# Decay rows inside the FoX score product, two heads scored ahead of the last value piece, pool products ahead of the values, a new depth order of the output projection

## The chip, the cores and the metric

One NeuronCore of a Trainium2 chip runs the whole program. The metric is the device time of one execution in microseconds (us), and the time of a kernel is the median of its runs.

## The reference

The reference is a two-layer decoder trunk over 256 tokens of width 1024. Each layer runs a token mixer, cross-attention into 256 memory tokens, and a SwiGLU channel mixer (dense in layer 0, the best 2 of 8 experts in layer 1). Every sub-layer has an RMSNorm before and after it. The change touches the token mixer only:

```python
proj = hn @ w_in
sq, sk, sv, fq, fk, fv, f_logit, u = jnp.split(proj, SPLIT_POINTS, axis=-1)
sb   = stick_breaking_attention(sq, sk, sv)             # 6 heads of 64
log_f_cum = cumsum(log_sigmoid(f_logit + b_forget))     # one row per FoX head
# FoX head: softmax_s( (q_t . k_s)/8 + log_f_cum[t] - log_f_cum[s] ), s <= t, times v
fox  = forgetting_attention(fq, fk, fv, log_f_cum)      # 6 heads of 64
pool = multiscale_pool(u, pool_w, pool_scale)           # 4 causal windows, 64 channels each
return concatenate([sb, fox, pool]) @ w_out
```

A stick-breaking head takes z = q.k/8, forms log_keep = -softplus(z) below the diagonal, sums it over the later keys, and weights the values with exp(log_sigmoid(z) + that sum).

## The kernel before

**Stages and banks.** Every product of a layer is a stage of tiles of 256 columns, listed in `STAGES` (L64); a mixer layer runs mixT (transposed, normalised tokens), u (pool input), f (forget logits), fqk and sqk (queries and keys, transposed), v (values, 6 tiles), the heads, pool (2 tiles), out (8 tiles). `ORDER` (L69) numbers the tiles, and tile n uses PSUM bank n mod 8. `pieces` (L1650) issues a stage on TensorE: per tile eight depth blocks `k` of 128, each three matmuls (high x high, high x low, low x high parts of the fp32 operands, L1626 to L1628 in `product`). ScalarE and VectorE move finished tiles out of PSUM, alternately (`take`, L774 and L1161; `plain_tile`, L405).

**Weights.** A weight piece (1 MB, two tiles) goes by DMA from SyncE's queue into one of six raw buffers. ScalarE writes its fp32r high part and VectorE the low part (`split`, L732 and L1156, the operations L730 and L1152), each into one of three buffers. `split_behind` places the split of piece c+3 behind the moves of piece c's tiles. SyncE waits at piece 14 (the first of xk) until the heads are mixed, then loads the post-norm gain, the memory tokens, and piece 14 on (L617 to L620).

**Heads.** `heads` stands once on TensorE (L1676), once on ScalarE (L809) and once on VectorE (L1215); each engine works in its own written order, and semaphores tie them together. In iteration i:

- TensorE: the scores of FoX head i (L1689: queries x keys over 64 rows; L1692: `decay_q` x `decay_k` over 128 rows, which adds the two decay terms to the same bank), the scores of stick-breaking head i (L1697, L1698), the sums of head i-1 (L1706 to L1708), the transposes of the FoX probabilities of head i-1 (L1714), the value products of head i-2 (L1726, L1727).
- ScalarE: Abs, Exp, Ln of head i (L816 to L818), the two softmax exponentials (L821), the Exp of the stick-breaking weights of head i-1 (L827), the move of its transposed probabilities (the helper L730), and in every second iteration the high parts of a finished pair (L730 again, output `rows`).
- VectorE: mask and row maximum of FoX head i (L1224, L1227), keep terms (L1231, L1233), reciprocal and scaling (L1235, L1237), the logarithms of the weights of head i-1 (L1246), and in every second iteration the low parts of a pair (L1152, output `rows`).

Six heads of each kind run through this in eight iterations per layer. TensorE enters `heads` after all v tiles are moved; ScalarE and VectorE enter it behind the moves of v and behind the split that `take_all` puts after the last v tile. `decay_q` and `decay_k` lie in `xn`; GpSimd clears them and writes the constant rows (L662 to L666), VectorE writes the decay rows in `decay` (L1201).

**After the heads.** TensorE waits for `sb_mix` and `fox_mix` (the last low parts), runs the two pool products (L2042), waits until both pool tiles are split (`wait_moved`, L2044), and begins `out`, whose tiles take the depth blocks in the order 0 to 7. Blocks 0 to 2 are stick-breaking pairs, 3 to 5 FoX pairs, 6 and 7 the pool. GpSimd prepares the pool input (L677 to L687) and signals `pool_ready`.

## Time and profile before

| | us |
|---|---|
| median of 3 runs | 1666.8 |
| lowest and highest run | 1658.07, 1669.35 |
| the profiled execution | 1652.1 |
| its span, first to last instruction | 1650.3 |
| mean granted TensorE clock in the span | 0.98 |

The profile comes from one execution. Its times count from the start of the span; a busy time is the time an engine spends in instructions, and "idle before" is its pause ahead of an instruction with the engine that ended it. The first layer's mixer lies at about 5 to 145 us, the second's at about 475 to 600 us. Matmul ends are modelled, so differences between starts are firmer than single durations. In a timeline "xN" counts records; a plain fp32 matmul has two.

### The profile page before, as it was taken

The numbers are of one execution on the slowest core, as the hardware profiler recorded it, in microseconds if no ns is written. First come the engines' busy times: TensorE is split into PE (matmuls) and PEld (weight loads), VectorE is DVE, ScalarE is ACT, GpSimd is POOL, SyncE is SP. The second block draws the span as 40 slices with busy tenths as digits, with TensorE's granted clock in tenths as the row PEclk, the third lists the DMA queues.
The fourth block names the chain that finished last, engine by engine and source line by source line (L and its number), as shares of the span: only waits on it lengthen the run. The fifth ranks groups of instructions, "written<-read, shape, count | busy, mean of one in ns | idle before, by whom it ended". The sixth has DMA issues, their size and how long they took to land.

```text
span 1650.3 us, 23029 instructions
## 1 busy us (share of the span) xinstructions
PE 1508.8 (91%) x9225; PEld 1301.8 (79%) x9225; DVE 1102.0 (67%) x1052; ACT 962.3 (58%) x1108; POOL 131.9 (8%) x125
## 2 busy tenths in 40 slices
PE   6989988999979899879999998989898899999986
PEld 6969978999979699779997676666666799866664
DVE  4556545444555565466776888878798676778886
ACT  5356445334353664354445787868778454478776
POOL 6100000000040000001001002020200200100200
PEclk9999998999989999979999999999999999999998
DMA  9318523555633085334667999999999667689993
GB/s 312 113 60 260 184 85 128 179 182 189 200 102 103 25 270 192 115 103 154 230 230 241 322 382 341 377 352 347 385 341 374 232 222 246 236 288 382 354 370 146
DMA packets 224150, 385.79 MB, mean 234 GB/s; under 512 B 11924, under 2 KB 114680, under 8 KB 223880
## 3 DMA queue, kind: packets, MB, share of 16 engines
q1 hardware_dynamic: 223072, 382.12, 66.3%
q8 instruction: 83, 1.36, 0.3%
q10 hardware_dynamic: 424, 1.08, 0.2%
q0 software_dynamic: 512, 0.74, 0.2%
q14 instruction: 59, 0.48, 0.1%
HBM read 382.85 MB, written 1.05 MB: 233 GB/s over the span
## 4 chain that ended last, share of the span: by engine, by line
PE 74%; DVE 12%; ACT 8%; issue 4%; DMA 1%; ACTq 0%; SPq 0%; DVEq 0%
PE banks L1626 12%; PE banks L1627 12%; PE banks L1628 12%; DVE w_low L1152 9%; PE banks L1624 8%; PE banks L1625 7%; PE banks L1937 6%; ACT w_high L730 5%; PE banks L1939 5%; PE banks L1881 2%; PE banks L1873 2%; PE banks L1832 1%; PE banks L1818 1%; DVE after_heads L1424 1%; ACT rows L730 1%
## 5 line engine op out<-in xcount | busy, mean ns | idle before, releaser
L1152 DVE TENSOR_TENSOR w_low<-raw,w_high 128x2048 fp32r<-128x2048 f32 x357 | 808.2, 2292 | 302.7 <-ACT w_high L730 295.9
L730 ACT ACTIVATE w_high<-raw 128x2048 fp32r<-128x2048 f32 x357 | 679.9, 1915 | 279.1 <-PE banks L1939 102.0
L1624 PE MATMUL banks<-w_high,rows 128*128 128x512 f32 (+1 forms) x576 | 224.4, 396 | 30.9 <-DVE w_low L1152 20.9
L1626 PE MATMUL banks<-rows,w_high 128*128 128x256 f32 x832 | 238.3, 286 | 12.2 <-DVE rows L1153 8.6
L1627 PE MATMUL banks<-rows,w_high 128*128 128x256 f32 x832 | 237.6, 286 | 0.0
L1628 PE MATMUL banks<-rows,w_low 128*128 128x256 f32 x832 | 237.4, 285 | 0.0
L1625 PE MATMUL banks<-w_low,rows 128*128 128x512 f32 (+1 forms) x576 | 213.3, 377 | 1.5 <-issue 1.5
L1937 PE MATMUL banks<-rows,w_high 128*128 128x320 f32 x704 | 186.4, 310 | 8.3 <-DVE w_low L1152 5.6
L1939 PE MATMUL banks<-rows,w_low 128*128 128x256 f32 x704 | 184.6, 279 | 0.0
L1626 PEld LDWEIGHTS banks<-rows,w_high 128*128 128x128 f32 x832 | 162.0, 195 | 14.2 <-issue 13.7
L1624 PE MATMUL banks<-w_high,eT 128*128 128x512 f32 x352 | 144.3, 410 | 20.4 <-DVE w_low L1152 13.6
L1624 PEld LDWEIGHTS banks<-w_high,rows 128*128 128x128 f32 x576 | 109.2, 190 | 67.9 <-issue 38.9
L1627 PEld LDWEIGHTS banks<-rows,w_high 128*128 128x128 f32 x832 | 162.1, 195 | 0.4
L1628 PEld LDWEIGHTS banks<-rows,w_low 128*128 128x128 f32 x832 | 161.9, 195 | 0.0
L1626 PE MATMUL banks<-w_high,rows 128*128 128x256 f32 x480 | 136.5, 284 | 5.1 <-DVE rows L1152 2.8
L1937 PEld LDWEIGHTS banks<-rows,w_high 128*128 128x128 f32 x704 | 132.8, 189 | 9.3 <-issue 9.3
L1625 PE MATMUL banks<-w_low,eT 128*128 128x512 f32 x352 | 138.9, 395 | 0.0
L1627 PE MATMUL banks<-w_low,rows 128*128 128x256 f32 x480 | 135.8, 283 | 0.0
L1628 PE MATMUL banks<-w_high,rows 128*128 128x256 f32 x480 | 135.8, 283 | 0.0
L1939 PEld LDWEIGHTS banks<-rows,w_low 128*128 128x128 f32 x704 | 134.0, 190 | 0.5 <-issue 0.5
L1625 PEld LDWEIGHTS banks<-w_low,rows 128*128 128x128 f32 x576 | 109.4, 190 | 22.4 <-issue 5.5
L1624 PEld LDWEIGHTS banks<-w_high,eT 128*128 128x128 f32 x352 | 66.0, 188 | 64.7 <-issue 38.3
(200 smaller groups left out, 2028.8 us busy)
## 6 DMA issues: line engine op xcount, KB each, us to landing
raw<-in_moe_w_gate_dram SPq DMA_DIRECT2D x176, 512.0 KB, 5.4
raw<-in_moe_w_up_dram SPq DMA_DIRECT2D x176, 512.0 KB, 5.6
raw<-in_moe_w_down_dram SPq DMA_DIRECT2D x176, 512.0 KB, 5.4
raw<-in_w_in_dram SPq DMA_DIRECT2D x40, 512.0 KB, 6.1
raw<-in_xa_wkv_dram SPq DMA_DIRECT2D x32, 512.0 KB, 8.5
raw<-in_dense_w_gate_dram SPq DMA_DIRECT2D x22, 512.0 KB, 4.4
raw<-in_dense_w_up_dram SPq DMA_DIRECT2D x22, 512.0 KB, 4.2
raw<-in_dense_w_down_dram SPq DMA_DIRECT2D x22, 512.0 KB, 3.6
```

Of the source, the lines that this page charges most:

```text
L730: return act.activation(out_, in_, ACT.Copy, scale=scale)
L1152: return dve.tensor_tensor(out_, in_, plain(high), ALU.subtract)
L1424: dve.tensor_tensor(both, both, banks[:, at:at + blocks, 0:width(s)], ALU.mult).then_inc(hidden_ready, 1)
L1624: pe.matmul(dst, stay[0], move[0], start=start, stop=False, skip_group_check=True)
L1625: return pe.matmul(dst, stay[0], move[1], start=False, stop=stop, skip_group_check=True)
L1626: pe.matmul(dst, stay[0], move[0], start=start, stop=False, skip_group_check=True)
L1627: pe.matmul(dst, stay[0], move[1], start=False, stop=False, skip_group_check=True)
L1628: return pe.matmul(dst, stay[1], move[0], start=False, stop=stop, skip_group_check=True)
L1873: pe.matmul(banks[:, bank_of(half, s, blocks - 1, blocks), 0:width(s)], fold, low_rows[:, half, 0:width(s)], start=False, stop=True, skip_ ...
L1881: ins = pe.matmul(dst[:, j, b * P:(b + 1) * P], inner[:, b, j * P:(j + 1) * P], twice if stacked(b) else ident, start=True, stop=True)
L1937: pe.matmul(dst[:, 0:2 * n].rearrange("p (h s) -> p h s", h=2), w_h[:, k, cols], x[:, :, 0:n], start=(i == 0 and k == 0), stop=False, skip ...
L1939: ins = pe.matmul(dst[:, 0:SEQ], w_l[:, k, cols], x[:, 0, :], start=False, stop=(i == of_step(s) - 1 and k == per - 1), skip_group_check=True)
```

## The change

Six edits, in both layers:

1. **FoX scores in one product.** `fox_q` and `fox_k` have 128 rows per head: 64 rows of queries or keys, and in the other half the decay rows, ones and zeros. `plain_tile` moves each fqk tile in two halves of 64 rows into them. One pair of products replaces L1689 and L1692. GpSimd clears four strided halves and writes two sets of ones, VectorE's `decay` writes 12 rows instead of 7.
2. **Order inside a head's scores.** The stick-breaking scores come ahead of the FoX scores on TensorE (`head_front`).
3. **Two heads ahead.** The fronts of heads 0 and 1 run on all three engines after v tile 3, ahead of v tiles 4 and 5. `heads` begins at iteration 1. The split behind v tile 3 goes between the two fronts, the split behind v tile 5 behind the heads. Banks are counted from the first pool tile (`head_bank`).
4. **Where TensorE waits for v.** It waits for v tiles 0 and 1 ahead of the fronts and for all v tiles ahead of iteration 2.
5. **Pool products** move from behind the heads to between sqk and v, with their moves.
6. **Depth order of out:** 0, 1, 3, 4, 6, 7, 2, 5. The waits for the last `sb_mix` and `fox_mix` stand ahead of blocks 2 and 5 of its first tile.

```diff
-STAGES = [("mixT", 4), ("u", 2), ("f", 1), ("fqk", 6), ("sqk", 6), ("v", 6), ("pool", 2), ("out", 8),
+STAGES = [("mixT", 4), ("u", 2), ("f", 1), ("fqk", 6), ("sqk", 6), ("pool", 2), ("v", 6), ("out", 8),
...
+MIXED_IN_ORDER = [k for k in range(KT) if k % PAIRS < PAIRS - 1 or k >= 2 * PAIRS] + [PAIRS - 1, 2 * PAIRS - 1]
...
-        decay_q = view(flat_xn, 0, HEADS, SEQ)
-        decay_k = flat_xn[:, HEADS * SEQ:(HEADS + 1) * SEQ]
+        fox_q = view(flat_xn, 0, HEADS, SEQ)
+        fox_k = view(phase, 0, HEADS, SEQ)
...
+            if stage == "fqk":
+                for h in (2 * (i % PAIRS), 2 * (i % PAIRS) + 1):
+                    ins = move((fox_q if i < PAIRS else fox_k)[own_rows(h), h, :], src[own_rows(h), :],
+                               HD ** -0.5 if i < PAIRS else 1.0)
+                return ins
...
+        def own_rows(h):
+            return slice(HD * (h % 2), HD * (h % 2) + HD)
+        def decay_rows(h, at):
+            first_row = HD - HD * (h % 2) + at
+            return slice(first_row, first_row + HEADS)
+        def head_bank(layer, b):
+            return banks[:, (tile(layer, "pool") + b) % BANKS, :]
...
-                chain(pool.memset(flat_xn[:, 0:(HEADS + 1) * SEQ], 0.0))
+                for odd in range(2):
+                    for t in (fox_q, fox_k):
+                        chain(pool.memset(t[own_rows(1 - odd), odd:HEADS:2, :], 0.0))
                 for h in range(HEADS):
-                    chain(pool.tensor_scalar(decay_q[32:32 + HEADS, h, :], ones[32:32 + HEADS, :],
...
+                    at = decay_rows(h, 32)
+                    chain(pool.tensor_scalar(fox_q[at, h, :], ones[at, :], ident[at, at.start + h:at.start + h + 1], None,
+                                             ALU.mult))
+                chain(pool.memset(fox_k[decay_rows(0, 0), 0:HEADS:2, :], 1.0))
+                pool.memset(fox_k[decay_rows(1, 0), 1:HEADS:2, :], 1.0).then_inc(decay_set, 1)
...
 # ScalarE and VectorE
-                take_all(layer, "v")
+                take_all(layer, "pool")
+                take_all(layer, "v", 0, 3)
+                take(layer, "v", 3)
+                head_front(layer, 0)
+                split_behind(layer, "v", 2)
+                head_front(layer, 1)
+                take_all(layer, "v", 4, last_split=False)
                 heads(layer)
-                take_all(layer, "pool")
+                split_behind(layer, "v")
                 take_all(layer, "out")
...
 # TensorE
+                        if stage == "out" and i == 0 and k in (PAIRS - 1, 2 * PAIRS - 1):
+                            pe.wait_ge(sb_mix if k == PAIRS - 1 else fox_mix, PAIRS * (layer + 1))
...
+            def head_front(layer, i):
+                rows, c, n = own_rows(i), i // 2, HEADS * layer + i
+                sq, sk = (qkT[rows, PAIRS * m + c, :] for m in (2, 3))
+                b = head_bank(layer, 2 + i % 3)
+                pe.matmul(b[:, 0:SEQ], sk[:, 0:P], sq, start=True, stop=False, skip_group_check=True)
+                pe.matmul(b[:, SEQ:TRI], sk[:, P:SEQ], sq[:, P:SEQ], start=False, stop=False,
+                          skip_group_check=True).then_inc(sb_scored, 1)
+                b = head_bank(layer, i % 2)
+                if i >= 2:
+                    pe.wait_ge(fox_masked, n - 1)
+                for t, cols, keys in ((0, slice(0, P), P), (1, slice(P, TRI), SEQ)):
+                    ins = pe.matmul(b[:, cols], fox_q[:, i, t * P:(t + 1) * P], fox_k[:, i, 0:keys], start=(t == 0),
+                                    stop=(t == 1), skip_group_check=True)
+                ins.then_inc(fox_scored, 1)
...
+                    if i == 1:
+                        wait_moved(pe, after(layer, "v"))
...
-                pieces(layer, "v", x_parts)
-                if layer == 0:
-                    pe.wait_ge(consts_in, 16)
-                heads(layer)
                 pe.wait_ge(pool_ready, layer + 1)
...
                 for c in range(COUNT["pool"]):
                     pe.matmul(bank(tile(layer, "pool", c))[:, 0:SEQ], poolw[:, layer, c, :], pool_r[:, c, :],
                               start=True, stop=True).then_inc(tile_full, 1)
-                wait_moved(pe, after(layer, "pool"))
+                pieces(layer, "v", x_parts, of=range(4))
+                wait_moved(pe, tile(layer, "v", 2))
+                pe.wait_ge(decay_ready, layer + 1)
+                head_front(layer, 0)
+                head_front(layer, 1)
+                pieces(layer, "v", x_parts, of=range(4, COUNT["v"]))
+                heads(layer)
                 pieces(layer, "out", mix_parts)
```

ScalarE's and VectorE's `head_front` are the lines that stood under `if i < HEADS` of their `heads`, with `head_bank` for the bank. The loops of `heads` run over i = 1 to 7 and call it for i from 2 to 5.

## Rows read from the trace of the kernel before

**Rows 1.** The page, part 4: chain that ended last, by engine.

```profile
PE 74%; DVE 12%; ACT 8%; issue 4%; DMA 1%; ACTq 0%; SPq 0%; DVEq 0%
```

**Rows 2.** Windows, layer 0's heads: length, busy (xcount) PE, PEld, DVE, ACT, POOL, clock, DMA, GB/s.

```profile
79.50:117.70 38.20, 32.91 (x178) 23.37 (x179) 23.82 (x75) 24.53 (x64) 0.00 (x0) 1.00 0.03 9
```

**Rows 3.** Timeline, ScalarE, moves of v tiles 3 and 5: start, us, instruction, idle before.

```profile
73.49 0.38 ACT L730 ACTIVATE phase<-banks 128x256 f32<-128x256 f32 x1 [3.58 <-PE banks L1628]
...
79.24 0.38 ACT L730 ACTIVATE phase<-banks 128x256 f32<-128x256 f32 x1 [3.57 <-PE banks L1628]
```

**Rows 4.** Critical chain, 55 to 125 us: start, us, what.

```profile
79.52 1.91 ACT w_high L730
81.46 2.29 DVE w_low L1152
...
88.06 0.85 PE banks L1692 x4
...
98.02 0.85 PE banks L1689 x4
...
103.41 0.85 PE banks L1689 x4
```

**Rows 5.** Timeline, start of the heads on TensorE and VectorE.

```profile
79.73 0.89 PE L1689 MATMUL banks<-phase 64*128 64x128 f32 x4 [0.52 <-issue]
...
81.40 0.48 PE L1697 MATMUL banks<-phase 64*128 64x256 f32 x1
...
81.42 0.49 PE L1689 MATMUL banks<-phase 64*128 64x128 f32 x2
...
85.89 0.55 DVE L1237 TENSOR_SCALAR phase<-phase,small 128x128 f32<-128x128 f32 x2
```

**Rows 6.** Timeline, ScalarE's Abs of heads 1 to 5, layer 0.

```profile
85.56 0.47 ACT L816 ACTIVATE phase<-banks 128x384 f32<-128x384 f32 x1
...
90.41 0.48 ACT L816 ACTIVATE phase<-banks 128x384 f32<-128x384 f32 x1
...
95.21 0.49 ACT L816 ACTIVATE phase<-banks 128x384 f32<-128x384 f32 x1
...
100.60 0.49 ACT L816 ACTIVATE phase<-banks 128x384 f32<-128x384 f32 x1
...
106.00 0.49 ACT L816 ACTIVATE phase<-banks 128x384 f32<-128x384 f32 x1 [0.55 <-PE banks L1698]
```

**Rows 7.** Timeline, one round of ScalarE and VectorE between two Abs.

```profile
92.04 0.56 DVE L1231 SCALAR_TENSOR_TENSOR phase<-banks,phase 128x384 f32<-128x384 f32 x1 [1.58 <-ACT phase L818]
...
93.76 0.55 DVE L1246 TENSOR_TENSOR phase<-banks,cst 128x384 f32<-128x384 f32 x1
...
94.35 0.52 ACT L827 ACTIVATE phase<-phase 128x384 f32<-128x384 f32 x1 [1.47 <-DVE phase L1246]
```

**Rows 8.** Timeline, TensorE from the last values to the first out tile.

```profile
114.11 0.38 PE L1727 MATMUL banks<-phase 128*64 128x128 f32 x2
115.47 1.10 PE L2042 MATMUL banks<-res,poolw 128*128 128x256 f32 x4 [0.98 <-DVE rows L1152]
117.70 0.35 PE L1626 MATMUL banks<-w_high,rows 128*128 128x256 f32 x1 [1.13 <-issue]
```

**Rows 9.** Timeline, GpSimd in layer 0's mixer, first and last step.

```profile
21.80 1.60 POOL L662 MEMSET xn<- 128x1792 f32 x1 [12.49 <-DMA cst<-in_constants_dram]
...
46.55 0.74 POOL L687 TENSOR_TENSOR res<-res 64x256 f32<-64x256 f32 x1
```

**Rows 10.** Timeline, SyncE's queue: the load of the memory tokens.

```profile
115.84 0.43 SPq L620 DMA_DIRECT2D phase<-in_mem_dram  x1
```

**Rows 11.** The memory tensor: time from issue to landing, both layers.

```profile
DMA to landing us min/median/max: 6.5/7.4/8.3
```

**Rows 12.** Timeline, ScalarE's first use of the memory tokens, layer 0.

```profile
130.38 1.06 ACT L745 ACTIVATE xn<-phase 128x1024 f32<-128x1024 f32 x1
```

**Rows 13.** Timeline, ScalarE's Abs of head 5, layer 1.

```profile
563.30 0.49 ACT L816 ACTIVATE phase<-banks 128x384 f32<-128x384 f32 x1 [0.55 <-PE banks L1698]
```

More of the change, by code:

```diff
@@ L828, in heads @@
                         act.wait_ge(fox_turned, n + 1)
[L829 removed]
+                        move(fox_pT[:, j % 2, :], head_bank(layer, 5)[:, 0:TRI]).then_inc(fox_pt, 1)
                     if i >= 2 and i % 2 == 1:
@@ L1241, in heads @@
+            def heads(layer):
+                for i in range(1, HEADS + 2):
+                    if 2 <= i < HEADS:
+                        head_front(layer, i)
+                    if i <= HEADS:
                         j, n = i - 1, HEADS * layer + i - 1
@@ L1648, in turn_stage, with pieces @@
                             ins.then_inc(tile_full, 1)
-            def pieces(layer, stage, tokens=None, x=x_parts, turned=None):
-                for i in range(COUNT[stage]):
+            def pieces(layer, stage, tokens=None, x=x_parts, turned=None, of=None):
+                for i in range(COUNT[stage]) if of is None else of:
                     if (stage, i) == ("out", 6):
```

150 lines of the change are left out of this document (70 added, 80 removed).

## The prediction

> **What bounds the kernel now.** I read the chain that ended last first. TensorE holds 74% of it, VectorE 12%, ScalarE 8%, DMA 1% [rows 1]. So a change counts where it shortens TensorE's work, or a place where TensorE waits for the two others. The next view is the table by windows. In the value stage ScalarE waits 3.58 and 3.57 us for TensorE at each second tile, and two tiles take 5.75 us [rows 3]: that stage is bound by products. The heads are another kind of stage: in 38.2 us TensorE is busy 32.9, VectorE 23.8, ScalarE 24.5, and DMA 3% [rows 2]. No engine is full, so the end is set by turns between engines, and the timelines must be read.
>
> They show three parts in layer 0. (a) The start. V ends at 79.2 (79.73 less the 0.52 of pause) [rows 5], and the first thing ScalarE and VectorE do is the split behind it, 1.91 and 2.29 us, until 83.75 [rows 4]. The chain runs through it, so both heads' elementwise work stands behind it. (b) The rounds. TensorE's own round is 103.41 - 98.02 = 5.39 us [rows 4]. ScalarE's Abs come at 85.56, 90.41, 95.21, 100.60, 106.00: steps of 4.85, 4.80, 5.39, 5.40. Only the last waited for TensorE by the view (0.55 us) [rows 6]. (c) The end. The last value product ends at 114.49 (114.11 + 0.38), the pool products wait until 115.47, and out begins at 117.70 [rows 8].
>
> The second layer does the same 457.3 us later (563.30 against 106.00) [rows 6, 13], so each saving counts twice.
>
> **Why the rounds have a second bound.** Between two Abs stand, one behind the other: Abs, Exp, Ln on ScalarE (VectorE's L1231 waits 1.58 us for them), then four VectorE steps up to L1246 at 93.76, then L827 at 94.35, which waited 1.47 us for L1246, then a move and the next Abs at 95.21 [rows 6, 7]. That is a ring of 4.80 us in which TensorE's products have no part as long as scores and sums come in time. A round with a pair's high parts is longer by 5.39 - 4.80 = 0.59.
>
> **The change part by part (layer 0, times on the scale of before).**
>
> Decay rows in the score product. L1692 goes, 0.85 us of TensorE per head [rows 4]. What replaces L1689 has 128 rows instead of 64. No row shows this product itself; the nearest are L1689 over 64 rows and L1692 over 128, both 0.85 for the same columns [rows 4]. So I take 0.85 saved, with the other end at 0 (the joined product costs as much as both; it replaces them with half the instructions, which excludes a loss). TensorE's round becomes 5.39 - 0.85 = 4.54. The ring of 4.80, or 5.39 with a pair, then binds. Of six times 0.85 = 5.1 us nearly all is lost to it: in the rounds that end with Abs 3, 4 and 5 the ring gives 4.80, 5.39, 4.80 against 4.80, 5.39, 5.40, a saving of **0.6**.
>
> Here a rule speaks against the joining. L1697 of head 0 (rows 0 to 63) and L1689 of head 1 (rows 64 to 127) start 0.02 us apart [rows 5]: they run side by side. The Trainium skill (TensorE: Matmul & The Clock Gate, The mechanism) says that products in different row groups of the array run at the same time. The trace agrees. A product over all 128 rows can share with nobody, so by the rule the two first fronts took five slots of 0.85 before and take four now: one slot less, not two.
>
> More rows for others. Every fqk tile is moved in two halves instead of one, VectorE writes five decay rows more, GpSimd makes four half clears for one (1.60 us) [rows 9] and two sets of ones for one. ScalarE's pause of 3.58 us in such stages [rows 3] hides the moves. GpSimd finishes at 47.29 (46.55 + 0.74) [rows 9]; if each new clear costs as much as the whole old one, that is 4.8 us more, some 52. I cost it at 0; what it costs if the cover goes is the third rival.
>
> Pool products first. They take 1.10 us in the trace [rows 8]. Now they stand ahead of v, which TensorE binds, so v tile 3 ends at 79.21 - 5.75 + 1.10 = 74.56 instead of 73.46 [rows 3, 5]. Their moves fall into the pauses of rows 3. The upper end is 1.6, with a pause at the change between kinds of product like the 0.52 of rows 5, the lower 0.9.
>
> Two heads ahead. Fronts begin at 74.56 + 0.52 = 75.08. Stick-breaking scores of head 0 end at 75.93, FoX at 76.78, the second head's at 78.48. V tiles 4 and 5 then run to about 78.8 + 5.75 = 84.5. For head 0 the trace has 85.56 - 83.75 = 1.81 us from VectorE's start on the mask to the end of ScalarE's softmax part [rows 4, 6], so ScalarE is through with it at 76.9 + 1.81 = 78.7 (its Abs, Exp and Ln lie before and beside that). Split of piece 11: high until 80.65, low until 82.95. From the end of the low part (83.75) [rows 4] to the scaled probabilities (86.44) [rows 5] it was 2.69 us with the same work, so head 1 is through at 85.65. Then one v move (0.35) and L1246 of head 0 at 86.0. From L1246 to the next Abs it is 95.21 - 93.76 = 1.45 [rows 6, 7]. Abs 2 comes at 87.45, before at 90.41: **2.95 saved**, pool's 1.10 already paid. TensorE needs for it: v tile 5 done at 84.6, sums and transposes of head 0 (at most 1.5, half of what is left of its round of 5.39 after three groups of 0.85), the scores of head 2, 0.85: 86.9, in time by 0.5. Here is the added wait: ahead of head 2's scores TensorE waits for v tile 4's move, which stands in VectorE's queue behind head 1, at 86.0 by the estimate; behind the wait stand the scores of head 2, and Abs 2 waits for them. The lower end of the saving is 1 (this queue 2 us late), the upper 4 (the split hidden wholly).
>
> The split behind v tile 5 goes behind the heads: 1.91 + 2.29 in ScalarE's and VectorE's queues as out begins. Its piece serves out tiles 4 and 5, two pieces of 5.75 us after out begins; it is done after 4.6. It delays the first tile's post-norm part by some 1.5 us, which nothing waits for before the banks come round, so 0.
>
> The tail. From Abs 5 to the last value product it was 114.49 - 106.00 = 8.49 us, all turns of ScalarE, VectorE and TensorE, and none of them is edited. So it ends at 114.49 - 2.95 - 0.6 = 110.94.
>
> New depth order. Before, 117.70 - 114.49 = 3.21 us lay between the last value product and out. Now out begins at once, with 0.25 for the step. Six blocks of three products at 0.12 us (48 in 5.75) [rows 3] last 2.2 us. The last low part ends TensorE's pause ahead of the pool products, at about 115.4 [rows 8], 0.9 after the values. Block 2, 2.2 behind them, finds it done. **2.95 saved** (2.2 to 3.2).
>
> What goes on behind: the memory tokens' load is released by the end of the heads, 3.55 earlier, but used by ScalarE 6.5 earlier. Issued 115.84, landed 6.5 to 8.3 later, so at 124.1 at worst, used at 130.38 [rows 10 to 12]: the slack shrinks from 6.3 to 3.3 and nothing waits. The weights queue behind this load, so they too come 3 us closer to their use; they would have to be the bound in out or xk to cost anything, and DMA has 1% of the chain [rows 1].
>
> **Sum.** 2.95 + 0.6 + 2.95 = 6.5 us per layer, 13.0 for both. 1652.1 - 13.0 = 1639.1 for the profiled execution (its span 1650.3 and 1.8 around it), a ratio of 0.9921. The median of the runs is 1666.8, 14.7 above that execution; against it the forecast is 1666.8 x 0.9921 = **1653.7**. A measurement of this kernel tells about 1% (16.7 us) from no change, so the likeliest case lies inside "same". Its own range: the bounds of the parts give 1 + 0 + 2.2 to 4 + 0.6 + 3.2, 3.2 to 7.8 per layer, 1651 to 1660.
>
> **Rivals.**
>
> *TensorE binds the rounds after all.* Then each of the four later fronts gives its full 0.85 on top: the chain that ended last does run over TensorE's groups from 88 to 103 [rows 4], which speaks for it. Against: steps of 4.85 and 4.80 in rows 6, where TensorE's round is 5.39, and the 1.47 us waits of L827. It needs a ring shorter than 4.80, for instance since stick-breaking scores come first. Price: rounds of 4.54 against 4.80, 5.39, 4.80, which is 1.4 more, and up to 1.05 at the start, 2.4 per layer: 1653.7 - 4.9 = 1649. Chance 0.15.
>
> *The start gives nothing.* The two fronts only shift the same split (one still lies between them, 4.2 us), and TensorE waits for v tile 4's move in VectorE's queue. Then only 0.6 + 2.95 less pool's 1.10 stays, 2.45 per layer: 1666.8 - 4.9 = 1662. For it: head 1's chain ends at 85.7, after v's end at 84.6, so TensorE has no head work ready beyond head 0's. Against: head 1's whole front was behind 83.75 before and is ready at the same time as head 0's now. Chance 0.17.
>
> *Slower: GpSimd is late for the pool products.* TensorE now needs `pool_ready` ahead of v, at 79.2 - 3 x 5.75 = 61.9, instead of at 115. All products wait behind it. It decides once GpSimd ends later than 61.9 + 6.5 = 68.4 in the first layer: 21 us later than 47.29. Each us beyond costs one. If the six strided clears and ones cost 6 us each instead of 1.6, GpSimd ends about 80: 18 - 6.5 = 11.5 slower in layer 0, about as much in layer 1, 1666.8 + 23 = 1690. The 1.60 us of the whole old clear [rows 9] speaks against it. Chance 0.04.
>
> *The rest*, such as a bank or a weight piece that comes late in out, a few us either way and within 1%: 0.04.
>
> **From these to the numbers.** Forecast 0.60, rivals 0.15, 0.17, 0.04, 0.04. Range: own range 1651 to 1660, widened to the first two rivals and to the spread of a median (runs of before lie 1658 to 1669): 1642 to 1664. Faster by over 1% needs a result below 1650.1: two thirds of the first rival (0.10) and a fifth of the forecast (0.12), where its parts or the median fall low: 0.22. Slower by over 1%: the slower rival, 0.04. Within 1%: the rest, 0.74.
>
> **What would show it.** After: Abs to Abs steps of 4.8, 5.4, 4.8 from head 2 on, none waiting for TensorE; no L1692; L827 still waiting about 1.47 for L1246. From the last value product to the first out product under 0.5 us, with no wait inside out's first tile. From the last sqk product to the first out product 6.5 less than before. Wrong if the Abs steps shrink to the 4.5 of TensorE's round, if TensorE waits over 1 us behind v tile 5, or if a pause stands ahead of the pool products.

## The result, and the profile after

| | before | after |
|---|---|---|
| median | 1663.6 us (4 runs) | 1642.2 us (4 runs) |
| lowest and highest run | 1658.07, 1669.35 | 1640.05, 1643.27 |
| profiled execution, its span | 1652.1, 1650.3 | 1643.3, 1641.4 |
| mean granted clock in that span | 0.980 | 0.972 |

The ratio is 0.9869, 95% interval 0.983 to 0.9909. The changed kernel run again beside 23 more runs of before gave 1642.5 us (1641.24 to 1643.0) against 1662.1, ratio 0.9884 [0.9858, 0.9911]. So the change is worth 1.2 to 1.3%: over 1% in both point values, though both intervals reach to just under 1%. The forecast was 1653.7 and "within 1%" with 0.74; its range of 1642 to 1664 begins where the result lies.

The two spans differ by 8.9 us only. They are single executions, and the one of before, at 1652.1, was faster than all four runs in the table. So the comparison is made piece by piece inside layer 0's mixer, where both traces have the full clock.

First TensorE's timeline of the changed kernel, from the pool products (L2084) through the two fronts (L1728, L1729 the stick-breaking scores, L1736 the joined FoX score product) to the first full round. Columns: start, us, instruction, idle before and what ended it.

```profile
61.90 1.02 PE L2084 MATMUL banks<-res,poolw 128*128 128x256 f32 x4
62.57 0.47 PE L1670 MATMUL banks<-w_high,rows 128*128 128x256 f32 x1
...
74.35 0.70 PE L1728 MATMUL banks<-phase 64*128 64x256 f32 x2
...
76.90 0.92 PE L1736 MATMUL banks<-phase,xn 128*128 128x128 f32 x4
77.47 0.47 PE L1670 MATMUL banks<-w_high,rows 128*128 128x256 f32 x1
...
85.44 0.67 PE L1728 MATMUL banks<-phase 64*128 64x256 f32 x2 [0.68 <-DVE phase L1179]
...
89.76 0.70 PE L1728 MATMUL banks<-phase 64*128 64x256 f32 x2
...
90.61 0.92 PE L1736 MATMUL banks<-phase,xn 128*128 128x128 f32 x4
91.37 0.59 PE L1750 MATMUL banks<-phase,cst 128*128 128x256 f32 x2
...
94.11 0.70 PE L1728 MATMUL banks<-phase 64*128 64x256 f32 x2
```

To be seen: from the first pool product to the next product of v it is 62.57 - 61.90 = 0.67 us, though the group is drawn 1.02 long (ends are modelled, starts are firm). The fronts begin at 74.35 without a pause and end at 77.47, 3.12 for two heads. In a round the joined product takes 91.37 - 90.61 = 0.76. After v the only wait is 0.68 us, for the move of v tile 4 (L1179), which stands in VectorE's queue behind head 1. TensorE's own round is 94.11 - 89.76 = 4.35.

ScalarE's Abs of the six heads and the Exp of the stick-breaking weights (L853) of one round:

```profile
75.31 0.49 ACT L837 ACTIVATE phase<-banks 128x384 f32<-128x384 f32 x1 [0.46 <-PE banks L1729]
79.86 0.46 ACT L837 ACTIVATE phase<-banks 128x384 f32<-128x384 f32 x1
86.59 0.48 ACT L837 ACTIVATE phase<-banks 128x384 f32<-128x384 f32 x1
91.33 0.48 ACT L837 ACTIVATE phase<-banks 128x384 f32<-128x384 f32 x1
95.26 0.52 ACT L853 ACTIVATE phase<-phase 128x384 f32<-128x384 f32 x1 [1.47 <-DVE phase L1282]
96.59 0.50 ACT L837 ACTIVATE phase<-banks 128x384 f32<-128x384 f32 x1
101.34 0.48 ACT L837 ACTIVATE phase<-banks 128x384 f32<-128x384 f32 x1
```

They answer to [rows 6, 7]. The steps from head 2 on are 4.74, 5.26, 4.75, where TensorE's round is 4.35: none of these three Abs waits for TensorE, and L853 waits for VectorE as before. The sum of the mixer, from the first out product (L1670) backwards, on TensorE:

```profile
101.59 0.52 PE L1758 MATMUL banks<-cst,phase 128*128 128x128 f32 x3 [0.49 <-ACT phase L754]
...
104.17 0.70 PE L1750 MATMUL banks<-phase,cst 128*128 128x256 f32 x2 [0.62 <-DVE phase L1264]
...
106.32 0.52 PE L1758 MATMUL banks<-cst,phase 128*128 128x128 f32 x3 [1.01 <-ACT phase L754]
107.05 0.62 PE L1773 MATMUL banks<-phase 128*64 128x256 f32 x2 [0.21 <-DVE rows L1184]
...
109.44 0.38 PE L1774 MATMUL banks<-phase 128*64 128x128 f32 x2
109.76 0.39 PE L1670 MATMUL banks<-w_high,rows 128*128 128x256 f32 x1
```

The first out product comes 117.70 - 109.76 = 7.94 us earlier than in [rows 8]. By pieces:

| piece of layer 0 | forecast | measured | from |
|---|---|---|---|
| start: third head's Abs | 2.95 | 3.82 | 90.41 against 86.59 |
| rounds: from there to the sixth Abs | 0.6 | 0.84 | 15.59 against 14.75 |
| tail: to the start of the last value product | 0 | 0.01 | 8.11 against 8.10 |
| end: from there to the first out product | 2.95 | 3.27 | 3.59 against 0.32 |
| sum | 6.5 | 7.94 | |

These are times from the start of the span, and the two executions do not reach the values at the same time. In before the first product behind sqk, the first of v, is this one; in after it is the pool product at 61.90, 0.13 later:

```profile
61.77 0.28 PE L1626 MATMUL banks<-w_high,rows 128*128 128x256 f32 x1
```

Counted from there the saving is 7.94 + 0.13 = 8.07 us. In layer 1, where the same products start at 519.07 and 512.85, it is (575.01 - 519.07) - (560.70 - 512.85) = 8.09, with Abs steps of 6.74, 4.73, 5.26, 4.75. So the mixers give 16.2 us. By layer 1's first out product the profiled execution is 575.01 - 560.70 = 14.3 us ahead, and at its end only 8.9. It has the lower mean granted clock, 0.972 against 0.980, and has lost some us in stretches at half clock. One of them stands at the start of xk (the keys of the memory tokens) in layer 0, behind a pause that before had too:

```profile
136.62 0.36 PE L1670 MATMUL banks<-rows,w_high 128*128 128x256 f32 x1 [1.82 <-issue]
...
137.68 0.42 PE L1670 MATMUL banks<-rows,w_high 128*128 128x256 f32 x1
137.89 0.41 PE L1671 MATMUL banks<-rows,w_high 128*128 128x256 f32 x1
...
140.70 0.28 PE L1670 MATMUL banks<-rows,w_high 128*128 128x256 f32 x1
140.82 0.28 PE L1671 MATMUL banks<-rows,w_high 128*128 128x256 f32 x1
```

From start to start it is 0.21 us, later 0.12. The same products in the trace of before, behind the same pause of 1.82 us, are at 0.12 at once:

```profile
144.53 0.35 PE L1626 MATMUL banks<-rows,w_high 128*128 128x256 f32 x1 [1.82 <-issue]
...
145.31 0.28 PE L1626 MATMUL banks<-rows,w_high 128*128 128x256 f32 x1
145.43 0.28 PE L1627 MATMUL banks<-rows,w_high 128*128 128x256 f32 x1
```

GpSimd, which the third rival was about, has four half clears of 0.73 for the one of 1.60 [rows 9] and ends at 50.7 instead of 47.3, 11 us before TensorE needs the pool input:

```profile
21.53 0.73 POOL L684 MEMSET xn<- 64x768 f32 x1 [11.75 <-DMA cst<-in_constants_dram]
...
24.75 7.48 POOL L687 TENSOR_SCALAR xn<-cst 6x256 f32<-6x256 f32 x6
...
32.29 0.73 POOL L689 MEMSET phase<- 6x768 f32 x1
...
48.04 2.67 POOL L711 TENSOR_TENSOR res<-res 64x256 f32<-64x256 f32 x1
```

### The profile page after: what moved, and what is told of

Same layout as the page of the kernel before. It is cut to its first block, busy times and chain, and to the rows that moved or that the text cites. A ratio compares the mean times of both kernels' runs of the same rounds, so it can differ in the third digit from the quotient of the medians.

```text
span 1641.4 us, 22961 instructions
## 1 busy us (share of the span) xinstructions
PE 1509.3 (92%) x9177; PEld 1307.6 (80%) x9177; DVE 1109.4 (68%) x1068; ACT 964.2 (59%) x1114; POOL 147.1 (9%) x133
## 3 DMA queue, kind: packets, MB, share of 16 engines
q8 instruction: 80, 1.31, 0.3%
## 4 chain that ended last, share of the span: by engine, by line
PE 73%; DVE 13%; ACT 10%; issue 4%; DMA 1%; ACTq 0%; SPq 0%; DVEq 0%
PE banks L1670 12%; PE banks L1671 12%; PE banks L1672 12%; PE banks L1668 9%; DVE w_low L1184 8%; PE banks L1669 7%; PE banks L1982 6%; ACT w_high L754 5%; PE banks L1984 5%; PE banks L1918 2%; PE banks L1926 2%; PE banks L1877 2%; PE banks L1863 1%; DVE after_heads L1462 1%; ACT rows L754 1%
## 5 line engine op out<-in xcount | busy, mean ns | idle before, releaser
L1670 PE MATMUL banks<-rows,w_high 128*128 128x256 f32 x832 | 239.0, 287 | 11.9 <-DVE rows L1185 8.3
L1670 PEld LDWEIGHTS banks<-rows,w_high 128*128 128x128 f32 x832 | 162.6, 195 | 13.9 <-issue 13.4
L1670 PE MATMUL banks<-w_high,rows 128*128 128x256 f32 x480 | 137.3, 286 | 2.8 <-DVE rows L1184 2.8
```

Source lines behind the costliest of these rows:

```text
L1670: pe.matmul(dst, stay[0], move[0], start=start, stop=False, skip_group_check=True)
```

## The experiments

In each, the start of the first out product of layer 0 is set against 109.76 of the changed kernel. Where the first head's Abs is later or earlier than 75.31, that offset comes from ahead of the heads and is taken off first; for the two kernels with all of v ahead of the heads it is read from the pool products, which start at 61.90 in the changed kernel. A comparison in layer 0 sees tenths of a us, the medians only whole ones.

### Both kernels again

Before, unchanged, gave 1660.7 (1654.7 to 1667.45, 12 runs), ratio 0.9992 [0.9968, 1.0017]; what after gave stands above. Their expectations:

> The kernel before unaltered, a second profile of it. Theory M: ratio 1.000 within 0.004; first out product at 117.7 us within 0.3; half-clock spells at other places or of other length than in the first profile, and a span that differs from 1650.3 by about half the difference in the length of these spells (mean clock lower by 0.005 goes with some 8 us more). Rival S: spells at the same places and the span within 2 us of 1650.3.

> The changed kernel unaltered, to separate what the edits give from what the runs of both kernels scatter. Theory M (the mixers give 2 x 7.9 us, read from the two profiles between the last sqk product and the first out product; what lies beyond is where TensorE's half-clock spells happen to fall): ratio to before 0.988 to 0.993, i.e. 12 to 20 us, and a profile whose first out product is again at 109.8 us while the later stages differ from the last profile by a few us either way. Rival S (the changed order also removes something systematic behind the mixer, worth 6 us): ratio 0.987 or lower again, and the stages behind the mixer shorter than in before at the same clock.

In the second trace of before the first out product is at 117.30, 0.4 earlier than in the first trace (I had allowed 0.3), as is all ahead of it; in that of after at 109.00, its first Abs at 74.56, both 0.75 earlier. Counted from the first product behind sqk, at 61.37 and 61.15, the second pair gives (117.30 - 61.37) - (109.00 - 61.15) = 8.08 us, the first gave 8.07. Behind the mixers the two pairs differ. The second changed execution is 574.65 - 559.44 = 15.2 us ahead at layer 1's first out product and 1657.4 - 1639.3 = 18.1 at the end, where the first pair had 14.3 and 8.9.

### Two heads ahead, undone

All six v tiles ahead of the fronts, as before the change. With them go both weight splits of v on ScalarE and VectorE, which again stand ahead of the fronts, and edit 4: TensorE waits for all v tiles ahead of the fronts. The four other edits are kept. TensorE's part:

```diff
-                pieces(layer, "v", x_parts, of=range(4))
-                wait_moved(pe, tile(layer, "v", 2))
+                pieces(layer, "v", x_parts)
+                wait_moved(pe, after(layer, "v"))
...
                 head_front(layer, 0)
                 head_front(layer, 1)
-                pieces(layer, "v", x_parts, of=range(4, COUNT["v"]))
```

> The changed kernel with edit 3 undone: fronts of heads 0 and 1 behind v tile 5 and behind its split, all else as changed. Theory M (start 3.8 us per layer of the 7.9): Abs of head 2 within 0.7 us of before's 90.41 on the same scale, first out product 3.5 to 4.5 us later than 109.8, so about 113.8; whole kernel 7 to 9 us slower than the changed one, ratio to before 0.994 to 0.997. Rival (the start gives nothing, the gain comes from the joined product and the order alone): first out product at 110 to 111.

1657.1 us (12 runs), ratio 0.9972 [0.9948, 0.9995]: nearly all of the gain is gone, more than I had put on this edit. The first out product comes at 116.35 (offset -0.20, so 6.8 us later), not at the 113.8 I had expected, and the steps of Abs are 4.23, 4.86, 6.55, 5.45, 4.75. The third head's Abs is already 4.8 late (91.19 + 0.20 against 86.59), and the rounds lose the other 2.0. The timeline of its TensorE shows why:

```profile
83.00 0.92 PE L1728 MATMUL banks<-phase,xn 128*128 128x128 f32 x4
86.51 1.22 PE L1742 MATMUL banks<-phase,cst 128*128 128x256 f32 x2 [2.59 <-DVE phase L1260]
...
89.16 1.22 PE L1720 MATMUL banks<-phase 64*128 64x256 f32 x2
```

and its table by windows (columns as in [rows 2], the clock is third from the right):

```profile
85.00:89.00 4.00, 2.49 (x9) 2.14 (x9) 3.79 (x15) 3.29 (x11) 0.00 (x0) 0.61 0.00 0
89.00:93.00 4.00, 4.00 (x12) 3.10 (x11) 1.86 (x8) 2.43 (x7) 0.00 (x0) 0.50 0.00 0
93.00:97.00 4.00, 4.00 (x17) 2.91 (x16) 2.55 (x9) 1.89 (x6) 0.00 (x0) 0.61 0.00 0
97.00:101.00 4.00, 4.00 (x25) 3.20 (x24) 2.27 (x9) 2.52 (x7) 0.00 (x0) 1.00 0.02 4
```

TensorE is through with both fronts at 83.92, while VectorE is still at the low part of the split (until 84.52). TensorE then has nothing to do for 2.59 us. In this pause, at about 85.9 (the clock is 1.00 from 85.0 to 85.5 and 0.50 from 86.0 on), the granted clock falls to its lower level, 1.2 GHz, and stays there for some ten us: the scores take 1.22 where they take 0.70 at 2.4 GHz. In the kernel before, TensorE pauses at the same place for 1.71 us, and there the clock stays at 1.00 [rows 2]. (The same pause and the same 1.22 stand in layer 1, at 544.43.) TensorE, with slack in these rounds at full clock, becomes their bound at half. The Trainium skill (TensorE: Matmul & The Clock Gate, Part 1: The HAM clock gate) says that the throttled clock is the default and that activity releases it. This trace agrees: the clock is back at about 96.1, with TensorE busy without a pause since 86.51.

The twelve runs tell the same: seven, with a mean granted clock of 0.962 to 0.966, have a median of 1660.1, and five, at 0.971 to 0.974, one of 1653.0. That fits spells which come in some executions and not in all, and cost some 7 us where they do. It isn't shown, as only one of the twelve was profiled.

Whether the pause is what brings it can be tried. So the same kernel with more work for TensorE: the joined FoX product issued twice, with the same result, since the second one starts the sums anew.

```diff
-                for t, cols, keys in ((0, slice(0, P), P), (1, slice(P, TRI), SEQ)):
-                    ins = pe.matmul(...)
+                for _ in range(2):
+                    for t, cols, keys in ((0, slice(0, P), P), (1, slice(P, TRI), SEQ)):
+                        ins = pe.matmul(...)
```

> The kernel with edit 3 undone (fronts behind v) and the joined product issued twice: more work for TensorE than in that kernel. There TensorE paused 2.59 us behind the two fronts and its granted clock fell to half for about 10 us in the heads of both layers, which put the first out product at 116.35. Clock theory: the 1.7 us of doubled products fill that pause to about 0.9 us, the clock stays at 1.00 through the heads, and the first out product comes at 113.5 to 115.0, earlier than with less work; median 1 to 5 us below that kernel's 1657.1. Rival (the half clock there had another cause): clock again at 0.5 and the first out product at 118 or later.

1650.5 us (8 runs), ratio 0.9949 [0.9927, 0.997]. The first out product is at 113.93 with an offset of -0.63, 2.0 earlier than without the extra products. The median is 6.6 us lower, but the intervals of the two ratios overlap and their series of before had medians of 1662.1 and 1659.7, so the 2.0 is the firmer figure (1.7 in layer 1, counted from its pool products). The pause is now half as long, 1.31 us shorter by two doublings of 0.65, and the clock stays whole:

```profile
83.23 1.58 PE L1729 MATMUL banks<-phase,xn 128*128 128x128 f32 x8
86.08 0.70 PE L1743 MATMUL banks<-phase,cst 128*128 128x256 f32 x2 [1.28 <-DVE phase L1260]
```

```profile
85.00:89.00 4.00, 2.92 (x17) 2.50 (x18) 3.79 (x14) 3.39 (x11) 0.00 (x0) 1.00 0.00 0
89.00:93.00 4.00, 3.77 (x24) 2.82 (x22) 2.41 (x10) 2.97 (x8) 0.00 (x0) 1.00 0.02 4
```

The extra products shorten the pause and also make TensorE busier ahead of it; which of the two keeps the clock up is not separated. Against the changed kernel it is 113.93 + 0.63 - 109.76 = 4.8 us per layer. In the changed kernel itself the doubling costs 1.6 (below), here less, as a part falls into the pause; so edits 3 and 4 together carry between 3.2 and 4.8 at full clock, and they also keep TensorE from that pause.

### The old depth order

The waits stay, ahead of blocks 2 and 5; only the order goes back to 0 to 7.

```diff
-MIXED_IN_ORDER = [k for k in range(KT) if k % PAIRS < PAIRS - 1 or k >= 2 * PAIRS] + [PAIRS - 1, 2 * PAIRS - 1]
+MIXED_IN_ORDER = list(range(KT))
```

> The changed kernel with the depth order of out back to 0 to 7, the waits ahead of blocks 2 and 5 kept, pool products still ahead of v. Block 2 then comes 0.7 us after the last value product instead of 2.2, and the last low parts of both kinds come about 0.9 later than that product. Theory M (most of the 3.2 us between values and out was the pool products and their split standing there): first out product still at 109.8 and a pause inside out's first tile of 0.3 to 0.8 us only, the kernel 0.5 to 1.6 us slower than the changed one in both layers together. Rival (the new depth order carries the saving): 3 us per layer lost, the second tile of out 3 us later.

1643.2 us, ratio 0.9897 [0.9868, 0.9925], first out product at 109.63, and no product of out's first tile waits. The low part of the last stick-breaking pair is done by the time block 2 comes, 0.8 us after the first product. The new order is worth nothing that can be seen. What took 3.27 us from the end is edit 5, the pool products and their split no longer standing there, together with the place of the waits, which this run keeps. In the changed kernel the very last low part is written from here on:

```profile
110.28 0.42 DVE L1184 TENSOR_TENSOR rows<-banks,rows 128x256 fp32r<-128x256 f32 x1 [0.23 <-ACT rows L754]
```

That is until 110.70, 0.94 behind the first out product. Before, TensorE stood still for such a part, 0.98 us ahead of the pool products [rows 8]. So about 1 of the 3.27 belongs to the moved waits and about 2.3 to edit 5. No run undoes either of them alone.

### TensorE's work in the rounds: the joined product twice

The same doubling in the changed kernel. I expected it to put back what edit 1 had taken out, 0.85 us per head.

> The changed kernel with each joined FoX score product issued twice into the same bank (the second overwrites the first, the values stay): it puts back the 0.85 us per head that edit 1 took from TensorE, and nothing else. Ring theory (ScalarE and VectorE bind the rounds at 4.74, 5.26, 4.75): TensorE's round goes from 4.35 to 5.20, the Abs steps of heads 2 to 5 become 5.2 to 5.3 each, the first out product comes at 111.2 to 111.8 instead of 109.8, and the kernel loses 3 to 4 us, far less than 12 x 0.85 = 10.2. TensorE theory (each product on TensorE is paid in full): first out product at 114.9, 10 us lost.

1645.7 us (1638.71 to 1650.28), ratio 0.9918 [0.989, 0.9946]. First out product at 110.94 with an offset of -0.38, so 1.6 per layer later; the steps from the third head on are 5.35, 5.54, 4.76. On TensorE:

```profile
91.54 1.58 PE L1737 MATMUL banks<-phase,xn 128*128 128x128 f32 x8
92.95 0.59 PE L1751 MATMUL banks<-phase,cst 128*128 128x256 f32 x2
```

From start to start the doubled product takes 1.41 where the single one takes 0.76, so the doubling adds 0.65 and not 0.85, and TensorE's own round is 5.00. Of 6 x 0.65 = 3.9 us per layer 1.6, two fifths, are seen. Where a round has 4.75 - 4.35 = 0.4 of slack on TensorE, 0.65 more costs part of itself. It fits the rounds' second bound, and the rival (each product counts in full, here 3.9) falls.

### What the second bound consists of: keep terms without the mask

VectorE's multiplication of the keep terms by the strict mask (L1264, 0.56 us) left out, in the changed kernel and in the one before. The output then misses this masking; the time is of the same program otherwise.

```diff
-                                               in1=sb_l[:, i % 2, :], op0=ALU.max, op1=ALU.add))
-                dve.tensor_tensor(sb_keep[:, i % 2, :], sb_keep[:, i % 2, :], strict, ALU.mult).then_inc(sb_kept, 1)
+                                         in1=sb_l[:, i % 2, :], op0=ALU.max, op1=ALU.add).then_inc(sb_kept, 1)
```

> The changed kernel without the masking of the keep terms (the multiplication by the strictly lower mask on VectorE is left out in every head). Ring theory: the ring shortens by 0.59 us, to 4.15, below TensorE's own 4.35; Abs steps of heads 2 to 5 become 4.35 to 4.4 where no pair's parts are moved and about 4.7 where they are, and the first out product comes 2 to 3 us earlier, near 107.3. TensorE theory: steps unchanged, first out product at 108.6 (only the two times at start and tail where the step stands alone).

> The kernel before with the same masking left out. Ring theory: TensorE's round is 5.40 there, so the rounds give nothing; only one step at the start (TensorE waits for the keep terms of head 0) and one in the tail go: first out product at 116.3 to 116.8 instead of 117.7, half or less of what the same cut gives in the changed kernel. Rival (VectorE binds before as well): 2.5 us or more.

Both expectations missed; each kernel ran once. In the changed kernel the first out product is at 109.49 with an offset of +0.27, 0.5 per layer earlier, and the steps are 4.70, 5.07, 4.62; in the one before the steps do not move (4.85, 4.80, 5.39, 5.40, as in [rows 6]) and the first out product, 117.33 with an offset of -0.19, is 0.2 earlier. VectorE's timeline of the first names the reason:

```profile
93.19 0.56 DVE L1262 SCALAR_TENSOR_TENSOR phase<-banks,phase 128x384 f32<-128x384 f32 x1 [0.38 <-ACT phase L839]
94.06 0.17 DVE L1265 RECIPROCAL small<-small 128x2 f32<-128x2 f32 x1 [0.32 <-ACT phase L842]
```

The reciprocal now waits for ScalarE's softmax exponentials (L842, the last ends at 94.04), which had run beside the keep terms and end nearly as late (in the changed kernel at 93.80, the keep terms at 94.11). The ring is real, but I had the wrong contents for its middle: Abs, Exp, Ln, then on ScalarE the two exponentials with keep terms beside them, then reciprocal, scaling, the logarithms of the weights (L1282), L853, a move, the next Abs. Taking out one of two branches of nearly equal length gives next to nothing.

### The ring made shorter

If so, the way out is to take L1282 out of the chain and not to make a link of it shorter: it needs only the sums of head i-1, which TensorE has long written. VectorE takes it ahead of head i's keep terms.

```diff
+                if i >= 2:
+                    take_sums(layer, i - 1)
...
-                    if i <= HEADS:
-                        j, n = i - 1, HEADS * layer + i - 1
...
-                        dve.tensor_tensor(sb_w[:, j % 2, :], head_bank(layer, 2 + j % 3)[:, 0:TRI], low_min,
-                                          ALU.min).then_inc(sb_logw, 1)
+                    if i <= HEADS and not 2 <= i < HEADS:
+                        take_sums(layer, i - 1)
```

> The changed kernel with one VectorE step moved: L1282 of head i-1 (the logarithms of its weights) comes ahead of the keep terms of head i instead of behind its scaled probabilities. The cut of the masking has shown that the keep terms are not the path: ScalarE's softmax exponentials run beside them and end as late. The ring through them is Abs, Exp, Ln, exponentials, reciprocal and scaling, L1282, L853, move: 4.74. Ring theory, corrected: taken early, L1282 lets ScalarE go on from its exponentials to L853 without the wait of 1.3 to 1.47 us; ScalarE's own round is then 3.5 to 4.2 and TensorE's 4.35 binds, so that the Abs steps of heads 2 to 5 become 4.35 to 4.6, the first out product comes 2 to 3.5 us earlier (106.3 to 107.8), and the kernel gains 4 to 7 us on the changed one's 1642.5. TensorE theory (rounds were bound by its products, nothing to gain): steps 4.74, 5.26, 4.75 as they are.

1637.4 us (1633.54 to 1637.82), ratio 0.9833 [0.9801, 0.9865], 5 us less than the changed kernel, though the intervals of the two just touch; first out product at 107.01 with an offset of +0.39, 3.1 per layer earlier. ScalarE's timeline:

```profile
93.86 0.51 ACT L853 ACTIVATE phase<-phase 128x384 f32<-128x384 f32 x1
...
95.46 0.49 ACT L837 ACTIVATE phase<-banks 128x384 f32<-128x384 f32 x1 [0.17 <-PE banks L1733]
...
99.81 0.49 ACT L837 ACTIVATE phase<-banks 128x384 f32<-128x384 f32 x1 [0.72 <-PE banks L1733]
```

L853 no longer waits, Abs now waits for TensorE, and the steps are 4.12, 4.35, 4.35: the last two are exactly TensorE's own round. Only here does the work that edit 1 removed come through nearly in full: the three steps are 12.82 us together, 2.77 less than in [rows 6], and TensorE's three rounds are 3 x 1.04 = 3.12 shorter.

### The split between the two fronts

The split of piece 11 behind both fronts and behind v tile 4's move, instead of between the fronts.

```diff
+                head_front(layer, 1)
+                take(layer, "v", 4)
                 split_behind(layer, "v", 2)
-                head_front(layer, 1)
-                take_all(layer, "v", 4, last_split=False)
+                take(layer, "v", 5)
```

> The changed kernel with the split of the weight piece behind both fronts instead of between them, and v tile 4's move ahead of it. By the chain that ended last the start runs through this split (1.9 + 2.3 us) and head 1's terms behind it. If so: Abs of head 2 at 85.8 instead of 86.6, TensorE's pause of 0.68 ahead of head 2's scores gone, first out product 0.6 to 0.9 us earlier, 1.2 to 1.8 in both layers, less than the runs can tell. If the start is bound by TensorE (v tiles 4 and 5, then sums): nothing moves.

1645.9 us (1641.69 to 1649.58), ratio 0.989 [0.9857, 0.9923]. Head 1's Abs comes 2.75 after head 0's instead of 4.55, and TensorE's wait of 0.68 goes; still the first out product is at 109.98 with +0.54 of offset, 0.3 per layer earlier, less than the 0.6 to 0.9 expected. VectorE:

```profile
83.21 2.29 DVE L1185 TENSOR_TENSOR w_low<-raw,w_high 128x2048 fp32r<-128x2048 f32 x1 [0.72 <-ACT w_high L754]
85.42 0.55 DVE L1283 TENSOR_TENSOR phase<-banks,cst 128x384 f32<-128x384 f32 x1
```

TensorE has written the sums of head 0 by 84.99, but their logarithms (L1283) stand behind the split's low part until 85.42. Behind L1283 come ScalarE's L853, which waits 1.48 us for it, and the third Abs. So the split has left the way of head 1 and now stands in the way of head 0, and the start is still bound by VectorE's queue.

### Blocks of out in the pauses of the tail

On top of the last one: the pauses of 0.62 and 1.01 in the tail are filled with four depth blocks of out's first tile (0, 3, 6, 7), whose rows are ready by then. The depth order of all out tiles becomes 0, 3, 6, 7, 1, 4, 2, 5, and the first tile later leaves out the four. In `heads`:

```diff
+                        if i == HEADS:
+                            early_blocks(layer, EARLY[1:])
...
+                    if i == HEADS - 1:
+                        pe.wait_ge(fox_masked, HEADS * layer + HEADS - 1)
+                        early_blocks(layer, EARLY[0:1])
```

> The last kernel with, besides, four depth blocks of out's first tile (0, 3, 6, 7) issued in TensorE's pauses of the tail: one behind the values of head 3, three between the sums and the transposes of head 5. The tail is 8.4 us of turns in which TensorE pauses 0.62 and 1.01 us and the blocks take 4 x 0.36. If pauses are free: the first product of out behind the last values comes at the same time, but the first tile ends 1.1 to 1.4 us earlier; with the split moved 1.8 to 2.3 us per layer, 4 us in all on the changed kernel. If the blocks push sums or transposes: no gain beyond the split's.

1635.7 us (1632.83 to 1637.46), ratio 0.9829 [0.9797, 0.986]. On TensorE:

```profile
104.93 0.37 PE L1673 MATMUL banks<-w_high,rows 128*128 128x256 f32 x1
...
105.97 0.28 PE L1675 MATMUL banks<-w_high,rows 128*128 128x256 f32 x1
106.19 0.52 PE L1776 MATMUL banks<-cst,phase 128*128 128x128 f32 x3
```

The transposes come at 106.19 without their pause of 1.01, and the four blocks (12 products of 0.12) are done for nothing. By the weight split behind them in `out` (115.14 with an offset of +0.18, against 116.71), layer 0 is 1.75 us ahead of the changed kernel, 1.4 of it above the kernel with the split alone. The median is 6.8 lower than the changed kernel's 1642.5; what goes beyond two times 1.75 is not in the mixers. Its runs have mean granted clocks of 0.973 to 0.978, those of the changed kernel 0.971 to 0.975.

### All three together

The shorter ring, the split behind both fronts and the early blocks.

> The three edits together: VectorE's logarithm step ahead of the keep terms (the shorter ring), split 11 behind both first heads, and four depth blocks of out's first tile in TensorE's pauses at the end of the heads. Theory A (the pauses of the tail come from the turns between ScalarE and VectorE and stay when the ring is shorter): the gains add, 3.1 of the ring and 1.4 to 1.8 of the early blocks per layer, some 9 us less than the changed kernel, ratio 0.977 to 0.980, median 1631 to 1633. Theory B (with the shorter ring TensorE sets the rounds, so the early blocks mostly displace other products): steps Abs to Abs of 4.35 as in the kernel with the shorter ring alone, tail pauses under 1 us in all, the gain of the ring plus at most 0.8 per layer, ratio 0.981 to 0.984, median 1635 to 1638. I hold B a little likelier, since the kernel with the shorter ring alone has pauses of under 1 us behind its last front.

1637.7 us (1631.52 to 1640.1, 5 runs), ratio 0.9844 [0.9818, 0.9869]. In the mixer the gains do add a little: that split of layer 0's `out` comes 4.1 us earlier than in the changed kernel, against 2.8 with the shorter ring alone. The heads began 0.05 and 0.39 later than the changed kernel's, so it is 4.1 against 3.1, 1.0 per layer above the shorter ring: a little over the 0.8 of theory B, far from the 1.4 to 1.8 of theory A. The last two steps are TensorE's 4.35 again. Yet the median is no lower. Its profiled execution is 7.2 us ahead of the changed kernel's through layer 1's mixer and 2.9 at the last weight split, with a mean granted clock of 0.970 against 0.972, and 0.978 in the one with the early blocks. The intervals of the three versions overlap; each beats both kernels, and none is shown to be the best.

## Why the prediction was right or wrong

**Right.** The bound: none of the three rounds' Abs waits for TensorE, steps of 4.74, 5.26, 4.75 against the 4.80, 5.39, 4.80 forecast, where TensorE's round fell by 1.04 to 4.35 (4.54 forecast). So the first rival is out, and most of edit 1's products were lost to the ring, as said. The tail kept its length to 0.01 us. The second rival is out: the start gave 3.82. GpSimd was never late. The memory tokens' load is issued 4.7 us earlier (111.17 against [rows 10]) and first used at 122.47, 7.9 earlier than in [rows 12], with no wait; the slack over the longest landing time of [rows 11] is 122.47 - 111.17 - 8.3 = 3.0, against 3.3 forecast.

**The step that failed: "two heads ahead", 2.95 forecast, 3.82 measured.** The mechanism held, and four sizes were off, all to one side. The pool products cost 0.67, start to start, not the 1.10 that the view draws as their length (and my lower end of 0.9 was outside). I set a pause of 0.52 ahead of the fronts, after [rows 5]; there is none, as edit 4 lets the fronts wait only for v tiles that were moved long ago. With 0.2 for the product's start the fronts begin at 74.35, not 75.08. The two fronts take 3.12, not 3.40, so v tile 4 begins at 77.47 where I had 78.8. And VectorE is through with head 1 and at v tile 4's move at 84.88, not at 85.65: the first split low part ends at 82.28, the estimate had 82.95. TensorE waits for that move, as forecast, for 0.68.

**The part that no term had.** The term above is the largest error of the sum, but not the largest part of the miss. From 1653.7 to 1642.2 it is 11.5 us: 3.2 as the median of before came out at 1663.6 with a fourth run, 3.1 as the mixers gave 16.2 and not 13.0, and 5.2 from outside the mixers, where the sum had put nothing. Only this last part carries the result beyond 1%, and its cause stays open (below).

**Two smaller terms.** The rounds gave 0.84, not 0.6: the ring is 0.05 shorter per round than before, and a pair's high parts cost 0.52, not 0.59. The end gave 3.27, not 2.95: no 0.25 for the step from values to out.

**A credit to the wrong edit.** I put the 2.95 of the end on the new depth order. The old order loses nothing; it is edit 5 that takes the pool products, their moves and their split out of the place between values and `out`, some 2.3 us, and the moved waits give about 1. The number came out near for another reason than the one given, which is luck.

**A wrong middle of the ring.** "Four VectorE steps up to L1246" took the keep terms for links. By the experiment without the mask they are one of two branches of nearly equal length. It did not change the sum, as the whole ring was taken from the trace, but it would have sent an engineer to shorten the wrong operation.

**From the sum to the time.** The mixers give 16.2 us, the forecast had 13.0. Against the median of before at the time of the comparison, 1663.6 and not 1666.8, 16.2 makes a ratio of 0.9903, inside both intervals at their upper ends. It would still have been within 1%. The medians say 21.4 and 19.6 us. The 3.4 to 5.2 us between are not located: of the two pairs of traces one shows 18.1 us at the end, the other 8.9. In the later series 56 runs of before lie between 1651 and 1675, and their time goes with the mean granted clock, from 1650.8 at 0.980 to 1675.2 at 0.965; the ten runs of after lie between 1640 and 1643 at 0.971 to 0.975. The 21 runs of before at 0.973 to 0.975 have a median of 1662.8, so the mean clock doesn't close the gap: it is 20 us at the same clock. Which stretches fall to half clock in which execution is seen in a profile only, and there are two for each kernel; that stays open. So the case that I held likeliest came out on the other side of 1%. That 1642.2 still lies in the range is luck as well: its lower end stood there for the first rival, which is out.

## What to carry to other kernels

Read the cost of a group of products from start to start, and when work moves, credit the saving to the place that becomes empty; then undo each edit alone, as two edits at one place are easily mixed up. Where the engines take turns, find the ring and test each link by leaving it out: a step with a branch of nearly the same length beside it is worth next to nothing, while moving one step out of the ring gave 3.1 us per layer here. And a pause of TensorE can cost beyond its length, since the clock may be halved behind it: here the kernel with the fronts behind v lost 2.0 us in layer 0 against itself with more products and a shorter pause.

## What the runs showed of the hardware that I had not expected

- In the profile of the kernel with the fronts not ahead, the clock fell to its lower level in a pause of 2.59 us on TensorE and stayed there for about ten us (0.50 of full speed by the windows), in both layers. With a pause of 1.28 us and more products ahead of it, it did not fall, nor with the 1.71 us of the kernel before. More work made this kernel's mixer 2.0 us shorter in layer 0 and 1.7 in layer 1.
- The same pause of 1.82 us at the start of xk is followed by products at 0.21 from start to start for three us in the first profile of after, and by products at 0.12 in that of before. In the second profile of after, the same kernel, the clock is 1.00 behind it too. So it depends on the execution and not on the kernel alone.
- GpSimd's clear of 64 rows by 768 columns takes 0.73 us, and so does writing ones to 6 rows by 768: the extra rows cost nothing there. Scaling 6 rows by 256 columns takes 7.48 for six, 1.25 each.
